# Value products of two heads in turns on the two column halves of TensorE, compressed values padded to 128 rows, another order in the first chunk

## The reference

```
# first block, chunked attention
p = jax.nn.softmax(sc, axis=-1)
return jnp.einsum('bhqk,bkhd->bqhd', p, v_c)
...
# second block, sparse attention: three weighted sums per head, and their gates
o_c = jnp.einsum('bhgqn,bhnd->bhgqd', p_c, vc)      # 15 compressed blocks a head
o_s = jnp.einsum('bhgqk,bhqkd->bhgqd', p_s, vsb)    # selected blocks
o_w = ...                                           # window
...
x = x + jnp.concatenate([o_nsa, o_sb], axis=-1) @ w_out
```

## Time and profile before

| what | value |
|---|---|
| median of 3 runs | 1222.62 us (1222.57 to 1224.28) |
| profiled execution, its own time | 1222.6 us |
| its span, first to last instruction | 1220.8 us |
| TensorE busy | 1208.5 us, 99% |
| DVE busy, ACT busy | 714.3 us (59%), 594.3 us (49%) |
| mean granted TensorE clock | 0.999 |

### The profile page before, as it was taken

The page is one execution under the profiler, slowest core; times in us unless marked ns, Lnnn a source line. Parts: engine busy times, 40 slices in busy tenths (PEclk is TensorE's granted clock), DMA queues, the critical chain, the costliest instruction groups (busy, mean ns, idle before and its releaser), DMA issues.

```text
span 1220.8 us, 15359 instructions
## 1 busy us (share of the span) xinstructions
PE 1208.5 (99%) x6189; PEld 1006.6 (82%) x6189; DVE 714.3 (59%) x966; ACT 594.3 (49%) x802; POOL 59.8 (5%) x101
## 2 busy tenths in 40 slices
PE   8999999999999999999999999999999998999998
PEld 6888888888889988888888888888997786888887
DVE  5666565554476766555447655456588747654452
ACT  6744454444354455444435544434548746543341
POOL 0100010000000000000004100000020001000000
PEclk9999999999999999999999999999999999999999
DMA  7744546544545444654453745453551222655530
GB/s 267 285 151 171 213 174 240 176 168 174 207 138 190 142 144 181 241 193 175 165 191 122 289 175 207 161 222 107 206 178 66 97 87 94 229 200 192 207 138 35
DMA packets 34687, 213.56 MB, mean 175 GB/s; under 512 B 4665, under 2 KB 6841, under 8 KB 10041
## 3 DMA queue, kind: packets, MB, share of 16 engines
q1 hardware_dynamic: 34617, 212.59, 48.3%
HBM read 211.53 MB, written 1.05 MB: 174 GB/s over the span
## 4 chain that ended last, share of the span: by engine, by line
PE 96%; DVE 2%; ACT 1%; DMA 0%; issue 0%; SPq 0%; POOL 0%; DVEq 0%; ACTq 0%; POOLq 0%
PE ps L320 29%; PE ps L322 28%; PE ps L321 28%; PE ps L326 4%; PE ps L806 2%; PE ps L765 1%; DVE wlo L1460 1%; DMA raw<-in_w_v 0%; PE ps L641 0%; ACT whi L1023 0%; DVE tmp L1478 0%; PE ps L623 0%; ACT xThi L1044 0%; ACT junk L1047 0%; PE ps L643 0%
## 5 line engine op out<-in xcount | busy, mean ns | idle before, releaser
L1460 DVE TENSOR_TENSOR wlo<-raw,whi 128x2048 fp32r<-128x2048 f32 (+2 forms) x200 | 440.5, 2236 | 113.2 <-ACT whi L1023 112.8
L1023 ACT ACTIVATE whi<-raw 128x2048 fp32r<-128x2048 f32 (+2 forms) x200 | 365.2, 1871 | 44.0 <-DMA raw<-in_w_gu 12.5
L320 PE MATMUL ps<-whi,xThi 128*128 128x512 f32 (+2 forms) x960 | 374.1, 390 | 4.6 <-DVE wlo L1460 2.8
L322 PE MATMUL ps<-whi,xTlo 128*128 128x512 f32 (+2 forms) x960 | 371.6, 387 | 0.0
L321 PE MATMUL ps<-wlo,xThi 128*128 128x512 f32 (+2 forms) x960 | 371.0, 386 | 0.0
L320 PEld LDWEIGHTS ps<-whi,xThi 128*128 128x128 f32 x960 | 180.7, 188 | 44.1 <-DVE wlo L1460 4.3
L1139 ACT ACTIVATE f_sil<-ps,stats 128x256 f32<-128x256 f32 x88 | 41.6, 473 | 359.0 <-PE ps L322 358.3
L322 PEld LDWEIGHTS ps<-whi,xTlo 128*128 128x128 f32 x960 | 180.5, 188 | 36.7
L321 PEld LDWEIGHTS ps<-wlo,xThi 128*128 128x128 f32 x960 | 180.8, 188 | 35.4
L1583 DVE SCALAR_TENSOR_TENSOR f_hid<-ps,stats,f_sil 128x256 f32<-128x256 f32 x88 | 42.4, 482 | 257.4 <-ACT f_sil L1139 257.2
L320 PE MATMUL ps<-whi,f_hThi 128*128 128x512 f32 x352 | 144.9, 412 | 0.0
(11 more groups left out here) (302 smaller groups left out, 1268.6 us busy)
## 6 DMA issues: line engine op xcount, KB each, us to landing
raw<-in_w_gu SPq DMA_DIRECT2D x88, 1024.0 KB, 5.8
raw<-in_w_dn SPq DMA_DIRECT2D x44, 1024.0 KB, 6.6
raw<-in_w_u SPq DMA_DIRECT2D x8, 1024.0 KB, 5.1
raw<-in_w_ao SPq DMA_DIRECT2D x8, 1024.0 KB, 6.5
raw<-in_w_v SPq DMA_DIRECT2D x6, 1024.0 KB, 6.0
raw<-in_w_bv SPq DMA_DIRECT2D x4, 1024.0 KB, 6.9
raw<-in_w_bk SPq DMA_DIRECT2D x4, 1024.0 KB, 5.6
raw<-in_w_bq SPq DMA_DIRECT2D x4, 1024.0 KB, 5.6
```

What stands on the lines that cost most here:

```text
L320: e.matmul(ps, a[0], b[0], start=start, stop=False)
L322: return e.matmul(ps, a[1], b[0], start=False, stop=stop)
L1023: e.activation(slots[slot_of[i]][0][:, cs], raw_cols(i, cs), ACT.Copy).then_inc(*inc("whi", i, p))
L1460: e.tensor_tensor(lo[:, cs], raw_cols(i, cs), hi[:, cs].bitcast(F32), ALU.subtract).then_inc(*inc("wlo", i, p))
```

## The change

Matmuls are issued in another order, some waits move, and one buffer is padded:

- `pv(i)` now does heads i and i + 1 together, matmul by matmul in turns, and waits for both copies first. The order is `pv(0)`, `turn_p(2)`, `turn_p(3)`, projection, `pv(2)`.
- `nsa_mix(f)` waits for both `npt`, then does the two heads in turns; `stick_mix` and the cross attention's `mix` take turns too. ACT's `turned_p(f, 0)` waits for the one signal at the end of `nsa_mix(f - 1)`, where it waited for head 0's.
- `vcmp` and the last 256 columns of `nPT` get 128 rows; POOL clears them once, and the products of the compressed values contract over 128 rows.
- In chunk 1 of v, the first half of the contraction is done for both tiles, then the second. ACT splits units 2 and 3 (and 4) earlier, ahead of `scaled_hi` of the second halves; DVE splits ahead of `scaled_lo`.

```diff
-                for t in range(2):
-                    e.wait_ge(*at("gelu", "v", c - 1, t))
-                    project(("v", c, t), GB[t], half_of(xT, t), pair, last=t)
+                for kts in (range(0, 4), range(4, 8)) if c == 1 else (range(8),):
+                    for t in range(2):
+                        if kts[0] == 0:
+                            e.wait_ge(*at("gelu", "v", c - 1, t))
+                        project(("v", c, t), GB[t], half_of(xT, t), pair, kts=kts, last=t)
...
-                def pv(j):
...
+                def pv(i):
+
+                    for j in (i, i + 1):
+                        e.wait_ge(*at(f"apt{j % 2}", g, j))
+                    if i == 0 and g:
                         e.wait_ge(*at("aolo", g - 1))
...
+                    for t, out, k, first, last in ((0, 0, 2, True, True), (0, 128, 0, True, False), (1, 128, 1, False, True)):
+                        for j in (i, i + 1):
...
                 pv(0)
                 turn_p(2)
-                pv(1)
                 turn_p(3)
                 ahead(steps, 1)
                 pv(2)
-                pv(3)
...
             def nsa_mix(f):
+
+                both = []
                 for j in range(2):
...
-                    steps = [[(vs[0], d[:, 512:640]), (vw[0], d[:, 640:768]), (vcmp[:, :], d[0:30, 768:896])],
...
+                    steps = [[(vs[0], d[:, 512:640]), (vw[0], d[:, 640:768]), (vcmp[:, :], d[:, 768:896])],
...
                     e.wait_ge(*at("npt", f, j))
...
+                for t in range(2):
+                    n = len(both[0][1][t])
+                    for i in range(n):
+                        for ps, steps in both:
+                            w, v = steps[t][i]
+                            m = e.matmul(ps[:, 128 * t:128 * t + 128], w, v, start=i == 0, stop=i == n - 1)
+                m.then_inc(*inc("product", "nmix", f))
...
             scaled_hi("g", 1, 0)
+            split(2)
             scaled_hi("g", 0, 1)
             split()
             scaled_hi("g", 1, 1)
-            split()
...
-            split()
             for c in range(4):
...
                 scale("g", t, 1, (XB, DB[0])[t][1], gain(0))
+                split()
                 scaled_lo("g", t, 1, xT)
-                split()
...
         heads("kc", (), 1, 30)
+        done(e.memset(vcmp[:, :], 0.0), "vcmp rows")
+        e.wait_ge(*at("turned", "k", 1))
+        for j in range(2):
+            done(e.memset(nPT[j][:, 768:1024], 0.0), "nPT rows", j)
```

More of the change, by code:

```diff
@@ L278, in block @@
     kcT = put("kcT", [128, 30])
-    vcmp = put("vcmp", [30, 64])
+    vcmp = put("vcmp", [128, 64])
     rb, rb8 = put("rb", [128, 256]), put("rb8", [128, 256])
@@ L632, in turn_p @@
                     turn(XB[j % 2], [a_s[j][:, 128 * i:128 * i + 128] for i in range(3)], "ap", g, j)
-                def pv(j):
[L635 to L639, removed]
-                        e.wait_ge(*at("aolo", g - 1))
-                    e.matmul(ps[:, 0:128], v[0], p[:, 2, :], start=True, stop=True)
-                    e.matmul(ps[:, 128:256], v[0], p[:, 0, :], start=True, stop=False)
-                    e.matmul(ps[:, 128:256], v[1], p[:, 1, :], start=False, stop=True).then_inc(*inc("product", "apv", g, j))
+                def pv(i):
+                    for j in (i, i + 1):
+                        e.wait_ge(*at(f"apt{j % 2}", g, j))
+                    if i == 0 and g:
+                        e.wait_ge(*at("aolo", g - 1))
+                    for t, out, k, first, last in ((0, 0, 2, True, True), (0, 128, 0, True, False), (1, 128, 1, False, True)):
+                        for j in (i, i + 1):
+                            ps = PS[7][64 * (j % 2):64 * (j % 2) + 64, 256 * (i // 2) + out:256 * (i // 2) + out + 128]
+                            m = e.matmul(ps, a_v[t][:, 256 * g + 64 * j:256 * g + 64 * j + 64], a_pT[j % 2][:, k, :], start=first, stop=last)
+                    m.then_inc(*inc("product", "apv", g, i))
                 turn_p(0)
@@ L796, in nsa_mix @@
                     ps = PS[0][64 * j:64 * j + 64, 0:256]
-                    steps = [[(vs[0], d[:, 512:640]), (vw[0], d[:, 640:768]), (vcmp[:, :], d[0:30, 768:896])],
-                             [(vs[0], d[:, 0:128]), (vs[1], d[:, 128:256]), (vw[0], d[:, 256:384]), (vw[1], d[:, 384:512]), (vcmp[:, :], d[0:30, 896:1024])]]
+                    steps = [[(vs[0], d[:, 512:640]), (vw[0], d[:, 640:768]), (vcmp[:, :], d[:, 768:896])],
+                             [(vs[0], d[:, 0:128]), (vs[1], d[:, 128:256]), (vw[0], d[:, 256:384]), (vw[1], d[:, 384:512]), (vcmp[:, :], d[:, 896:1024])]]
                     e.wait_ge(*at("npt", f, j))
[L800 to L807, removed]
+                    both.append((ps, steps))
+                e.wait_ge(*(at("olo", f - 1) if f else at("SV", 0)))
+                if f == 0:
+                    e.wait_ge(*at("vcmp"))
+                for t in range(2):
[5 more added lines that the diff above has]
+                m.then_inc(*inc("product", "nmix", f))
             def stick_mix(f):
@@ L812, in stick_mix @@
                     e.wait_ge(*at("SV", 1))
[L813 to L818, removed]
+                for t, out, cs, first, last in ((0, 0, 0, True, True), (0, 128, 128, True, False), (1, 128, 256, False, True)):
+                    for j in range(2):
+                        v = SV[t][:, 64 * (2 * f + j):64 * (2 * f + j) + 64]
+                        m = e.matmul(PS[0][64 * j:64 * j + 64, 256 + out:384 + out], v, L[f][:, j, cs:cs + 128], start=first, stop=last)
                 m.then_inc(*inc("product", "smix", f))
@@ L941, in mix @@
                     e.wait_ge(*at("mpt", t, f))
-                    for j in range(2):
-                        h = 2 * f + j
-                        for i in range(2):
+                    for i in range(2):
+                        for j in range(2):
+                            h = 2 * f + j
                             m = e.matmul(PS[bank][64 * j:64 * j + 64, 128 * f:128 * f + 128], vm[i][:, 64 * h:64 * h + 64], mPT[f][:, 2 * j + i, :], start=i == 0, stop=i == 1)
@@ L1315, in turned_p @@
                 e.activation(d[:, 512:768], PS[3][:, 0:256], ACT.Copy)
+                if f == 0:
+                    e.wait_ge(*at("pool", "nPT rows", j))
                 copy(d[0:30, 768:1024], PS[3][0:30, 256:512], "npt", f, j)
@@ L1323, in mixer @@
                 if f:
-                    e.wait_ge(*at("product", "nmix", f - 1, 0))
+                    e.wait_ge(*at("product", "nmix", f - 1))
                 turned_p(f, 0)
```

5 lines of the change are left out of this document (3 added, 2 removed).

## The result

The changed kernel takes 1211.12 us (median of 4 runs, 1209.72 to 1211.5), where the kernel before took 1223.11 us in the same session: a ratio of 0.9899, with a 95% interval of 0.9881 to 0.9916. It is faster by 12.0 us, where 12.3 were forecast; 1210.3 us was predicted. The span of the profiled execution went from 1220.8 to 1209.3 us.

What follows compares the result with a forecast made beforehand. TensorE was taken to bound the kernel, as long as the engines feeding it keep up. Mixer 7.4, attention 4.0 and first chunk 2.4, less 1.5 for the clock, make 12.3 us: 1222.6 to 1210.3 us, range 1204.5 to 1215.5.

Steps and rivals of the forecast that it cites:

- What a pass costs in turns: TensorE's two column halves work side by side: 0.11 us per two passes, plus 0.3 us to enter and leave.
- the overlap by half: Rival: passes in turns take 0.08 us each, losing 7 us of the gain; 1215 to 1217 us, chance 0.10.
- no overlap: Rival: passes in turns run one after the other at 0.11 us; about 1223 us, no change, chance 0.05.
- the slower rival: Each change of column half drains the array, at 0.14 us; about 17 us lost, 1239 us, chance 0.03.
- The moved wait: Mixer: TensorE waits for head 1's copy ahead of `nsa_mix`, 1.95, 1.9, 0 and 0.6 us; 7.4 of 12.4 us kept.
- The clock: Two mixer idles of 1.9 us may lower TensorE's clock; one fall taken, 1.5 us lost, bounds none and two.
- The rival with two falls: Mixer: the clock falls behind both long idles; 1211.8 us, chance 0.12.
- the forecast without a fall: Mixer: the clock stays up, so the mixer gives 7.4 us; 1208.8 us in total, chance 0.28.
- The attention: Value products of head pairs in turns at 0.9 us, and one entry saved: 1.0 us in each g, 4.0 in four.
- The first chunk: Wait for unit 3 shrinks to 0.5 us, a `gelu` wait of 0.4 comes: 2.4 us gained of 3.3 at stake.
- The gain kept whole: Rival: copies don't hold back TensorE's gain; 12.4 + 4.0 + 3.3 = 19.7 us saved, 1203 us, chance 0.07.
- The cross attention and the memsets: Cross attention already at 0.055 us a pass gains nothing; padding's memsets on POOL, about 0.3 us each, cost nothing.

Runs made afterwards that it cites:

- the first chunk as before: The changed kernel with whole-tile contraction in chunk 1 of v and the old order of unit splits on ACT and DVE, both restored; 1213.19 us in one run.
- the unit order of before: The changed kernel with units split on ACT and DVE in the old order, the contraction of chunk 1 still in halves; 1213.92 us, ratio 0.9924.
- the filled run: The changed kernel plus 8 unused identity products on TensorE ahead of the waits of `nsa_mix` at f = 0 and 1; 1209.0 us, ratio 0.9876.
- the run with the square sum earlier: The changed kernel with ACT and DVE copies and splits reordered in the mixer, plus tile 0's square sum ahead of a first-chunk split on ACT; 1204.46 us.
- Head after head: The changed kernel, padding kept, with `nsa_mix` doing one head after the other, each behind its own `npt` wait; 1211.46 us, ratio 0.9898.
- the copies and the splits in another order: The changed kernel with head 1's copy and stick exponential before the next exponentials, DVE's maximum earlier, and feed-forward weight splits moved on both engines; 1207.12 us.
- the run with the copy first: The changed kernel with ACT copying head 1's weights ahead of the stick exponential in each f; 1209.99 us, ratio 0.9892.
- the run with the copies ahead: The changed kernel with head 1's copy and the stick exponential before the next f's exponentials on ACT, and head 1's maximum earlier on DVE; 1209.89 us.
- 30 rows: The changed kernel with the products of the compressed values contracting over 30 rows again, still in turns; 1218.37 us in one run.

## Why the prediction came out right, and where it didn't

*What a pass costs in turns:* right. 0.055 to 0.06 us a pass and 2.55 us for 44 of them, where 2.6 were taken. This is the step that ruled out the overlap by half, no overlap, and the slower rival, whose mean would have been 0.10 us or more.

*The moved wait:* right in place, releaser and size: 1.93 us at f = 0 (1.95 forecast) and 0.59 at f = 3 (0.6). At f = 1 it was 1.50, not 1.9: the term was 0.4 too large, on the side of the loss. In the two runs whose clock didn't fall at f = 0 (the first chunk as before, the unit order of before) it was 1.79 and 1.80, so most of the difference is the fall at f = 0, which the working did not follow to f = 1: TensorE came later, and the copy less so.

*The clock:* the mechanism was right, the number of falls wrong. One fall was taken, two came. The rival with two falls stood at 0.12 and at 1211.8 us, and the 1211.12 measured are a little nearer to it than to 1210.3. The size of a fall was about right: the mixer takes 46.7 us without one (the filled run), 48.1 with one (the first chunk as before, the unit order of before) and 49.4 with two, so each costs 1.3 to 1.4 us, 2.7 in all where 1.5 stood in the sum. Without them the mixer gives 54.5 - 46.7 = 7.8 us, where the forecast without a fall had 7.4. With two it gave 5.1, where 5.9 were forecast.

*The attention:* 4.5 us, where 4.0 were forecast. The first pair takes 0.81 us, not 0.9, as the entry is shorter than the 0.3 taken; the second takes 391.79 - 390.89 = 0.90. The cover for the copies held.

*The first chunk:* 2.0 us between the two traces, 2.3 without the loads, where 2.4 were forecast. Unit 3 was split by 17.1 us (17.4 estimated), and the wait for it went altogether instead of shrinking to 0.5. The `gelu` cost 1.1 us in two waits and not 0.4 in one: ACT's square sums had moved behind an earlier split, which the working didn't follow. The run with the square sum earlier removed both waits. The 3.3 us at stake were mis-sized as well: the fall by itself cost next to nothing there (58.16 us with it, 58.07 without), while with all the waits gone the first chunk gave 58.16 - 54.19 = 4.0. So 2.4 came near the 2.3 by errors that cancel.

In the profiled executions the second fall cost 1.2 us more than the sum had and the first chunk gave 0.4 less; the waits and the attention gave 0.4 and 0.5 more. That makes 11.6 us where the sum had 12.3. The total, and the 12.0 between the medians above all, is closer than its terms, and that is luck.

*The gain kept whole* (1203 us) did not come, because ACT held the second head, as forecast. The rule of the Trainium skill (TensorEngine Tiling (Array Packing), PSUM Bottleneck), that tiling speeds up TensorE but not the copies out of PSUM, agrees with this trace: passes in turns ran at twice the rate, and 4.0 us of waits for copies out of PSUM appeared. That page expects it after a speedup of four; here it was two. But the runs add a limit to it. Head after head, with the same copies, `nsa_mix` had no idle ahead of it, so the wait came with asking for both copies at the start. And with the copies and the splits in another order, the same ACT and DVE kept 10.4 us of the 12.4. The bottleneck was when the copies came, not how fast they are.

*The cross attention and the memsets:* nothing, as forecast; the lead is the same to 0.1 us before and after the cross attention.

## What to carry to other kernels

When a change halves TensorE's work in a stage, look next at who feeds that stage, and in what order: here the copies, the exponentials and work for a later layer stood in one queue on ACT and on DVE, and moving the copies ahead and the work that was not urgent out of the way gave the mixer as much (5.4 us) as the change itself had kept (5.1). A wait moved from the second of two heads to the front costs its length and can cost the clock on top; padding without that wait gave the mixer the same. And a start in the profile is compared behind the first loads: these moved it by up to 1.9 us between runs of the same code. Where a gap on TensorE can't be closed, work that nobody needs may be cheaper than idling.

## What the runs showed of the hardware

The same idle did not always lower the clock. Behind 1.93 and 1.50 us in the changed kernel, 1.79 us at f = 1 in the run with the first chunk as before, 1.74 us in the run with the copy first and 1.82 us in the first chunk of before it fell to 1.2 GHz, and in the run with the copies ahead during an idle of only 1.09 us, which stood 1.1 us behind one of 1.28. Behind 1.93 us at f = 0 in the run with the first chunk as before, behind 1.92 us at f = 0 with the unit order of before, and behind 2.17 us at the start of the run with the square sum earlier it did not. Nor does the program decide it: of the 30 runs of the kernel before that were timed beside the experiments, 12 show a mean clock of 0.999 and 18 one of 1.000 (by an estimate, 3.4 us at half the clock make 0.9986 of the 1221 us). The length of an idle does not decide it alone; what else does is open.

How long it stays low varies more than the fall itself: 3.4 us behind the idle at f = 1 in the changed kernel, 6.8 us in the run with the copy first and about 13 us with 30 rows, while TensorE's records filled the time behind the idle in all three. A fall can thus cost 1.4 us or over 6.

A change between products over 128 and over 30 rows costs 0.14 us each way, at any order of the heads; a change of column half costs nothing that can be seen.

On TensorE, passes for the two column halves don't start strictly in the order written, which the words on the kernel before say of every engine. In its `stick_mix` all products of the first head stand ahead of the second head's, whose first pass starts at 945.74; the first head's last product (L818) starts only behind it:

```profile
945.96 0.27 PE L818 MATMUL ps<-x_L,x_SV 128*64 128x128 f32 x1
```
